# The first expert's tokens and the last pass's results moved by products instead of through memory, in a two-layer diffusion step on one core

## What is computed

```python
for l in range(2):
    xp, xs = layer_norm(ALPHA * x + gate * token_mixers(modulate(x))), ...   # conv and attention, both groups
    h = modulate(x)                                                # h for each group
    f = swiglu(h) if l == 0 else moe_swiglu(h)                     # layer 1: top 2 of 8 experts
    x = layer_norm(ALPHA * x + gate2 * f)

def moe_swiglu(h, router, wg, wu, wd):
    probs = softmax(h @ router); top_v, top_i = top_k(probs, 2); top_v = top_v / sum(top_v)
    gates = sum(one_hot(top_i, 8) * top_v[..., None], axis=-2)
    return sum(gates[..., e] * (silu(h @ wg[e]) * (h @ wu[e])) @ wd[e] for e in range(8))
```

## Time and profile before

| what | value |
|---|---|
| median of 3 runs | 1231.74 us (1231.68 to 1233.32) |
| profiled execution, its time | 1232.15 us |
| its span in the trace | 1230.3 us |
| TensorE (matmul) busy | 1129.3 us, 92% |
| VectorE, ScalarE, GpSimd busy | 852.8, 707.1, 133.7 us |
| moved | 336.78 MB, 274 GB/s |
| mean granted TensorE clock | 0.967 of full speed |

### The profile page before, as it was taken

How to read it: one execution, slowest core, us unless ns; L and a number is a source line. 1 busy time by engine, 2 the same in 40 slices (tenths; PEclk the granted TensorE clock), 3 DMA queues, 4 the chain that set the end, 5 groups by cost and what they waited for, 6 DMA issues and landing times.

```text
span 1230.3 us, 15641 instructions
## 1 busy us (share of the span) xinstructions
PE 1129.3 (92%) x5533; PEld 892.6 (73%) x5533; DVE 852.8 (69%) x1203; ACT 707.1 (57%) x1008; POOL 133.7 (11%) x142
## 2 busy tenths in 40 slices
PE   5699999999999999899999999379999999999980
PEld 1466667887788888766667887368878888888870
DVE  1575657767575455696657676358889889889965
ACT  1444545644644444544545645268888888888862
POOL 5040000001170000440000002220000000000001
PEclk9799999999999999999999999689999999999995
DMA  9799997665469656488775664179999999999952
GB/s 328 278 365 330 318 322 254 203 186 197 140 213 411 222 178 196 132 273 299 261 264 202 215 206 162 57 270 376 375 376 385 377 379 383 379 378 385 376 198 101
DMA packets 167064, 336.78 MB, mean 274 GB/s; under 512 B 6704, under 2 KB 27296, under 8 KB 167008
## 3 DMA queue, kind: packets, MB, share of 16 engines
q1 hardware_dynamic: 158288, 307.78, 71.0%
q0 software_dynamic: 8688, 28.25, 6.7%
q10 hardware_dynamic: 32, 0.01, 0.0%
HBM read 318.68 MB, written 17.33 MB: 273 GB/s over the span
## 4 chain that ended last, share of the span: by engine, by line
PE 84%; ACT 5%; DVE 5%; DMA 3%; issue 2%; POOL 0%; ACTq 0%; SPq 0%; DVEq 0%; POOLq 0%
PE bank L1310 24%; PE bank L1312 24%; PE bank L1311 24%; PE bank L1504 4%; ACT w_hi L568 2%; DMA raw<-in_ada_w 1%; PE bank L1567 1%; PE bank L1585 1%; DVE xT_lo L881 1%; PE bank L1459 1%; PE bank L1575 1%; ACT work L586 1%; DVE w_lo L846 1%; ACT xT_hi L591 1%; PE bank L1448 1%
## 5 line engine op out<-in xcount | busy, mean ns | idle before, releaser
L846 DVE TENSOR_TENSOR w_lo<-raw,w_hi 128x1024 fp32r<-128x1024 f32 (+1 forms) x492 | 571.3, 1190 | 191.7 <-ACT w_hi L568 189.6
L568 ACT ACTIVATE w_hi<-raw 128x1024 fp32r<-128x1024 f32 (+1 forms) x504 | 500.8, 1008 | 314.6 <-PE bank L1312 314.5
L1310 PE MATMUL bank<-w_hi,xT_hi 128*128 128x512 f32 (+1 forms) x1056 | 414.5, 392 | 18.4 <-DVE w_lo L846 12.3
L1312 PE MATMUL bank<-w_lo,xT_hi 128*128 128x512 f32 (+1 forms) x1056 | 403.1, 382 | 0.0
L1311 PE MATMUL bank<-w_hi,xT_lo 128*128 128x512 f32 (+1 forms) x1056 | 402.4, 381 | 0.0
L1310 PEld LDWEIGHTS bank<-w_hi,xT_hi 128*128 128x128 f32 x1056 | 200.4, 190 | 62.4 <-issue 14.2
L1312 PEld LDWEIGHTS bank<-w_lo,xT_hi 128*128 128x128 f32 x1056 | 199.1, 189 | 35.8
L1311 PEld LDWEIGHTS bank<-w_hi,xT_lo 128*128 128x128 f32 x1056 | 199.7, 189 | 31.1
L1310 PE MATMUL bank<-w_hi,hT_hi 128*128 128x512 f32 x360 | 141.8, 394 | 0.0
L1312 PE MATMUL bank<-w_lo,hT_hi 128*128 128x512 f32 x360 | 140.5, 390 | 0.0
L1311 PE MATMUL bank<-w_hi,hT_lo 128*128 128x512 f32 x360 | 140.3, 390 | 0.0
(11 more groups left out here) (236 smaller groups left out, 864.9 us busy)
## 6 DMA issues: line engine op xcount, KB each, us to landing
raw<-in_w_in SPq DMA_DIRECT2D x52, 1024.0 KB, 7.4
raw<-in_ada_w SPq DMA_DIRECT2D x48, 1024.0 KB, 7.5
raw<-in_moe_w_gate SPq DMA_DIRECT2D x32, 1024.0 KB, 7.4
raw<-in_moe_w_up SPq DMA_DIRECT2D x32, 1024.0 KB, 8.0
raw<-in_moe_w_down SPq DMA_DIRECT2D x32, 1024.0 KB, 7.8
raw<-in_moe_w_gate SPq DMA_DIRECT2D x16, 768.0 KB, 8.9
raw<-in_moe_w_up SPq DMA_DIRECT2D x16, 768.0 KB, 7.5
raw<-in_moe_w_down SPq DMA_DIRECT2D x16, 768.0 KB, 7.8
```

The lines of the kernel that those rows point to most:

```text
L568: nc.scalar.activation(w_hi[:, unit, 0:n], raw[:, r, at:at + n], ACT.Copy).then_inc(hi_done, 1)
L846: V.tensor_tensor(w_lo[:, unit, 0:n], raw[:, r, at:at + n], w_hi[:, unit, 0:n].bitcast(F32), ALU.subtract).then_inc(lo_done, 1)
L1310: pe.matmul(o, hi, wh, start=start, stop=False)
L1312: return pe.matmul(o, hi, wl, start=False, stop=stop)
```

## The change

- **First tokens.** Pass 0 no longer reads `x_rows`. A product with ones (`slot_mm`) gives every lane the numbers 1 to 128; VectorE compares them with each token's position in expert 0 (`first_tokens`, before `places`), which gives a 0/1 matrix per group; TensorE multiplies `tokens` by it, 16 products that leave the transposed rows where `gather` left them. The scatter stays, for passes 1 on, and SyncE waits for it three blocks later.
- **Route.** Experts are picked on the logits instead of the probabilities; the two gates follow from one exponential (`gates`), after pass 0's start. The transposes of group 0 go ahead of the router product.
- **Norm before the router.** Group 1's statistics go ahead of group 0's split; VectorE makes the four rests that GpSimd made. In layer 0 and at layer 1's start GpSimd's rests wait until group 0's scales exist.
- **Pass 0** stands ahead of the loop on ScalarE and VectorE too. SyncE takes every expert number from `plan`.
- **Last pass.** The gather of `y_rows` is issued when the pass before has been stored, so it runs beside the last pass; rows of the last pass are zero in memory. A 0/1 matrix times gate (`back_selected`, transposed on TensorE) brings the last pass's rows from `y_slot`: each of four banks takes a product of `best_y` with the identity and one of that matrix with `y_slot`.
- **Last norm and outputs.** Two fused operations per group in place of `xhat` and two; four halves of the output are sent by SyncE, which waits for them.

```diff
                 sp.wait_ge(x_sent, 16 * 2 * G)
-                x_load(0)
                 sp.wait_ge(gx_t, 1)
                 x_load(1)
 
@@ -396,14 +404,19 @@
 
                 expert(p * Q_EXPERT + q, of(e), between)
 
-            expert(q, of(0), first_rows)
-            with sp.Fori(1, NE - 1) as p:
-                one(p, p)
+            expert(q, of(0), first_rows, 2 * SLOTS)
             sp.wait_ge(plan_ok, 1)
             last_pass = sp.value_load(plan[0:1, 0:1], min_val=NE - 1, max_val=PASSES - 1)
-            with sp.Fori(NE - 1, last_pass + 1) as p:
-                one(p, sp.value_load(plan[0:1, bass.ds(p - (NE - 2), 1)], min_val=0, max_val=NE - 1))
-            y_store(last_pass, y_kept)
+            with sp.Fori(1, last_pass) as p:
+                one(p, sp.value_load(plan[0:1, bass.ds(p, 1)], min_val=0, max_val=NE - 1))
+            expert(last_pass * Q_EXPERT + q, of(sp.value_load(plan[0:1, bass.ds(last_pass, 1)], min_val=0, max_val=NE - 1)),
+                   lambda: y_store(last_pass - 1, y_kept))
+            for g in range(G):
+                for half in range(2):
+                    sp.wait_ge(x_ok, 2 * DEPTH + 2 * g + half + 1)
+                    sp.dma_start(out[g][0][:, half * COL:(half + 1) * COL], x[:, g, half * COL:(half + 1) * COL]).then_inc(stored, 16)
+            sp.wait_ge(kv_kept, 64 * DEPTH)
+            sp.wait_ge(stored, 16 * 2 * G)
...
-                rests(turn0[l] + Q_LAYER, 0)
                 if l == 0:
+                    pool.wait_ge(nmr_ok, G + 1)
+                    rests(turn0[l] + Q_LAYER, 0)
...
+                    pool.wait_ge(nmr_ok, G * 2 + 1)
                     rests(turn0[1], 0)
...
                     if j == 8:
-                        act.wait_ge(y_sent, p * 16 + 16)
+                        if last:
+                            act.wait_ge(y_kept, 16)
+                        else:
...
+                    if j == 7 and last:
+                        for g in range(G):
+                            act.wait_ge(y_in[0][g], 16)
+                            nc.scalar.activation(best_y[0][:, g, :], best_y[0][:, g, :], ACT.Copy, scale=rs[:, 3, g:g + 1])\
+                                .then_inc(y_gated, 1)
...
+                    act.wait_ge(slot_mm, 1)
+                    nc.scalar.activation(slot_no, bank[3][:, P:2 * P], ACT.Copy).then_inc(slot_ok, 1)
+                    for i, b in enumerate((6, 7, 4, 5)):
+                        act.wait_ge(xt_t, i + 1)
+                        nc.scalar.activation(tokens[:, i // 2, i % 2 * COL:(i % 2 + 1) * COL], bank[b][:, :], ACT.Copy)\
+                            .then_inc(xt_ok, 1)
...
+                    for i, picked in enumerate((sel_half, gx_t)):
+                        act.wait_ge(picked, 1)
+                        nc.scalar.activation(xT_hi[:, 4 * i:4 * i + 4, 0, :], four(bank[i]), ACT.Copy).then_inc(gx_hi, 1)
+                    one_pass(q0, 0, False)
                     act.wait_ge(plan_ok, 1)
                     last_pass = act.value_load(plan[0:1, 0:1], min_val=NE - 1, max_val=PASSES - 1)
...
+                else:
+                    statistics(1)
+                    modulate(n + 1, 0)
+                    scales(n + 1, 1)
+                    lo(q + 1, 0, (0, 1))
+                    modulate(n + 1, 1)
+                    modulated_rests(n + 1, 0)
                 modulated_rests(n + 1, 1)
...
+            def first_tokens():
+
+                dve.wait_ge(pos_mm, 1)
+                then(V.scalar_tensor_tensor(out=rs[:, 6, :], in0=bank[2][:, 64:64 + G * NE].rearrange("p (g e) -> p g e", g=G)[:, :, 0],
+                                            scalar=1.0, in1=one_hot[:, :, 0], op0=ALU.add, op1=ALU.mult))
+                dve.wait_ge(slot_ok, 1)
+                for g in range(G):
+                    ins = V.tensor_scalar(first_sel[:, g, :], slot_no, rs[:, 6, g:g + 1], None, ALU.is_equal)
+                ins.then_inc(sel_ok, 1)
...
+            def back_selected():
+
+                dve.wait_ge(slot_ok, 1)
+                for i in range(2):
+                    for g in range(G):
+                        ins = V.tensor_scalar(last_terms[:, i, g, :], slot_no, last_rel[:, i, g:g + 1], rs[:, 3 + i, g:g + 1],
+                                              ALU.is_equal, ALU.mult)
+                then(ins)
+                V.tensor_tensor(last_sel, last_terms[:, 0], last_terms[:, 1], ALU.add).then_inc(back_sel, 1)
 
...
+                    V.scalar_tensor_tensor(out=best_y[0][:, g, :], in0=best_y[1][:, g, :], scalar=rs[:, 4, g:g + 1],
+                                           in1=best_y[0][:, g, :], op0=ALU.mult, op1=ALU.add).then_inc(rows_summed, 1)
+                for g in range(G):
+                    for half in range(2):
+                        dve.wait_ge(back_mm, 2 * g + half + 1)
+                        at = slice(half * COL, (half + 1) * COL)
+                        ins = V.tensor_tensor(gate_bc[n % 2][g][:, at], bank[2 * g + half][:, :], gate_bc[n % 2][g][:, at], ALU.mult)
+                    then(ins)
                     then(V.scalar_tensor_tensor(out=x[:, g, :], in0=x[:, g, :], scalar=ALPHA, in1=gate_bc[n % 2][g],
...
+                dve.wait_ge(ld_ln, 32 * (2 * DEPTH + 1))
+                for g in range(G):
+                    dve.wait_ge(std_ok, G * (n + 1) + g + 1)
+                    V.reciprocal(rstd[:, g:g + 1], sd[:, g:g + 1])
+                    then(V.scalar_tensor_tensor(out=x[:, g, :], in0=x[:, g, :], scalar=mv[:, g, 0:1], in1=ln_gb[2 * DEPTH][:, 0, :],
+                                                op0=ALU.subtract, op1=ALU.mult))
+                    for half in range(2):
+                        at = slice(half * COL, (half + 1) * COL)
+                        V.scalar_tensor_tensor(out=x[:, g, at], in0=x[:, g, at], scalar=rstd[:, g:g + 1], in1=ln_gb[2 * DEPTH][:, 1, at],
+                                               op0=ALU.mult, op1=ALU.add).then_inc(x_ok, 1)
...
-                    rests_by_pool(q0, 0)
+                    first_tokens()
                     places()
                     gathered(0)
+                    lo(q0, 0, (2, 3))
+                    gates()
+                    one_pass(q0, 0, False)
                     last_pass = dve.value_load(plan[0:1, 0:1], min_val=NE - 1, max_val=PASSES - 1)
-                    with dve.Fori(0, last_pass) as p:
...
+                    def tokens_turned(g, banks):
+                        pe.wait_ge(mod_hi, G * 3 + g + 1)
+                        for k in range(KD):
+                            ins = pe.transpose(banks[k // 4][:, (k % 4) * T:(k % 4 + 1) * T], modulated[:, g, k, :], ident[:, :])
+                            if k % 4 == 3:
+                                ins.then_inc(xt_t, 1)
+
+                    tokens_turned(0, bank[6:8])
...
+                    idle_products(3, 0)
+                    pe.wait_ge(xt_ok, 2 * G)
+                    pe.wait_ge(sel_ok, 1)
+                    for k in range(KD):
+                        for g in range(G):
+                            ins = pe.matmul(bank[k // 4][:, (k % 4) * T:(k % 4 + 1) * T], tokens[:, g, k * P:(k + 1) * P],
+                                            first_sel[:, g, :], start=g == 0, stop=g == G - 1)
+                        if k == KD // 2 - 1:
+                            ins.then_inc(sel_half, 1)
...
+                    for g in range(G):
+                        pe.wait_ge(rows_summed, g + 1)
+                        for half in range(2):
+                            o = bank[2 * g + half][:, :]
+                            pe.matmul(o, ident[:, :], best_y[0][:, g, half * COL:(half + 1) * COL], start=True, stop=False)
+                            if g == 0:
+                                pe.wait_ge(y_ok, last_pass * 2 + (half + 1))
+                            pe.matmul(o, last_selT[:, g, :], y_slot[:, half * COL:(half + 1) * COL], start=False, stop=True)\
+                                .then_inc(back_mm, 1)
 
```

More of the change, by code:

```diff
@@ L448, in _ @@
                 then(pool.memset(iota[:, v:v + 1], float(v - NE)))
+            for v in range(1, NE):
+                then(pool.memset(plan_f[:, v:v + 1], float(v)))
             then(pool.memset(all_ones[:, :], 1.0))
@@ L540, in _ @@
                                             bass.IndirectOffsetOnAxis(ap=row_no[:, i, g:g + 1], axis=0)).then_inc(y_in[i][g], 16)
-            for g in range(G):
-                pool.wait_ge(x_ok, 2 * DEPTH + g + 1)
-                pool.dma_start(out[g][0], x[:, g, :]).then_inc(stored, 16)
-            pool.wait_ge(stored, 16 * G)
-            pool.wait_ge(kv_kept, 64 * DEPTH)
         @block.scalar
@@ L659, in one_pass @@
                         hi(nq, ns, (0, 1), n)
+                    if j == 2 and last:
+                        act.wait_ge(back_t, 1)
+                        nc.scalar.activation(last_selT, bank[5][:, 0:G * P].rearrange("p (g t) -> p g t", g=G), ACT.Copy)\
+                            .then_inc(back_ok, 1)
```

(32 more changed lines are left out.)

124 lines of the change are left out of this document (63 added, 61 removed).

## The result

The kernel after the change took 1197.31 us (1196.97 to 1200.21, 4 runs), the kernel before 1231.98 us (1231.68 to 1233.32, 4 runs): a ratio of 0.9724, 95% interval 0.9712 to 0.9735. The profiled execution took 1197.48 us, its span is 1195.7 (before 1230.3).

A forecast was written before the change was run, and what follows sets the result against it. TensorE was taken as the bound (47.89 of a 48.3 us pass). Terms -19.6 - 0.7 + 6.2 + 0.5 + 1.0 - 11.6 - 0.5 = -24.7 us gave 1207.0 by the median, own range 1203 to 1211, wider range 1200.5 to 1214.

The forecast's parts named there:

- Pass 0 outside the loop on two engines ... cost nothing visible: Moving pass 0 out of the loop costs nothing visible, since sequencers run ahead; uncovered, some 0.6 us each.
- SyncE's issues cost less than GpSimd's ... 1.0 (0 to 2): End of the span: SyncE's cheaper issues and a last piece of a quarter of the output win 1.0 us.
- Held rests: Two further norms: holding GpSimd's rests until `nmr` wins 0.5 us in all, though delayed rests meet the sum and `xT_lo`.
- Last pass, 0.5 and 1.0: Last pass: compares, sum, copy and transposes cost 0.5 us (0 to 1.5), the gather's transfers 1.0 (0 to 4.2).
- the wait for `raw`: Last pass: a wait for `raw` there was listed among the signs that the forecast is wrong; no size given.
- Norm before the router, route and products: Before pass 0: router product 4.8 us earlier, pass 0 starting at 788.8 against 808.41, 19.6 us earlier (17.5 to 21).
- make_x, 6.2: Pass 0: GpSimd's four operations, no longer covered, alternate with VectorE's rests and lose 6.2 us (0 to 9).
- The rival that the port costs nothing: Pass 0: TensorE keeps going beside make_x, so the 6.2 us loss is absent: 1200.8 us; chance 0.13.
- Warm start, -0.7: Pass 0's start: behind a short gap the first seven products avoid half rate, winning 0.7 us (0 to 1.4).
- Tail on the engines, -10.6: After the last product: VectorE ends at 1210.7 instead of 1221.33, 10.6 us earlier.
- transfers as the bound: Passes: scatter and gather take the weights' time, gather 4.2 us and scatter 1.5 in pass 0: 1211.7; chance 0.12.
- Half clock: Pass 0: beside make_x TensorE's clock halves for the rest of the pass, 34 us lost, 1241; chance 0.03.

The follow-up runs named there:

- e1: The kernel before, with one tiny Silu on ScalarE added ahead of its loop over passes: 1225.60 us, ratio 0.9952.
- e2: The kernel after, with pass 0 put back into the loop on ScalarE alone: 1204.31 us, ratio 0.9773.
- e3: The kernel after, with pass 0 back in ScalarE's loop and one tiny Silu ahead of that loop: 1199.09 us, ratio 0.9737.
- e5: The kernel after, with the four output transfers issued and waited for by GpSimd instead of SyncE: 1205.74 us, ratio 0.9783.
- e7: The kernel after, with outputs still issued by SyncE but waited for by GpSimd: 1202.85 us, ratio 0.9768.
- e4: The kernel after, without the two waits that hold GpSimd's rests: 1193.79 us, ratio 0.9696.
- e11: The kernel after, with SyncE storing the pass before last, which releases the gather, behind all the last pass's weight blocks: 1197.08 us, ratio 0.9721.
- e6: The kernel after, with outputs issued by GpSimd but waited for by SyncE: 1202.75 us, ratio 0.9759.
- e8: The kernel after, without GpSimd's four make_x operations, so the x that the last norm adds to is not computed: 1190.54 us, ratio 0.9662.
- e12: The kernel after, with GpSimd's rests not held, make_x paced in smaller operations and the gather released late: 1191.89 us, ratio 0.9678.
- e10: The kernel after, with make_x in eight operations of 512 columns, each released after another block of rests: 1197.78 us, ratio 0.9713.

## Why the prediction was wrong

The forecast was a gain of 24.7 us, and it was 34.7. The differences by stretch are start +0.7, pass 0 +0.3, six passes -5.95, last pass +1.1, tail on the engines -0.6, end of the span -5.5, together -9.95 beside the -24.7.

- **"Pass 0 outside the loop on two engines ... cost nothing visible"** is the step that failed. It gave 0 to an edit worth 6.0 us: the stretch of six passes fell by 5.95, and with the table loads put in or taken out the period moved by 1.0 us a pass (e1, e2, e3). I asked what the edit costs the sequencers and not what it changes in ScalarE's state at the loop's head. The rows were there to be read: two groups of table loads, seven times each, and 0.4 us of a pass in which TensorE was idle. I had called TensorE the bound at 47.89 of 48.30 us and never asked what the missing part waited for. This miss alone is larger than the 3.2 us by which the time lies below the range.
- **"SyncE's issues cost less than GpSimd's ... 1.0 (0 to 2)"**: 6.5. The term was priced by issue times and the size of the last piece. From GpSimd's last issue to the end of the span it was 8.7 us, while the page gave 2.9 us to the landing. The 5.8 between stood in the profile and belonged to GpSimd (e5 to e7). This miss, too, is larger than 3.2 us by itself.
- **Held rests, "0.5 won in all (bounds: 3 lost, 3 won)"**: 3.5 lost (e4), at the lower bound. That the sum and `xT_lo` would meet the delayed rests was written down; the value near zero was the mistake, for at layer 1's start there was only 0.7 us to win at `nmr` against two such meetings.
- **Last pass, 0.5 and 1.0**: 2.6, within the bounds (0 to 5.7). Some 2.3 of it is the gather's (e11), through ScalarE's waits for weights, the wait for `raw` that was named as a sign of being wrong; moving it does not help.

The other terms:

- **Norm before the router, route and products**: from `nmr` to pass 0's first product 26.4 us, forecast 27.6. The start came out at 789.03 against 788.8 because `nmr` itself began 1.4 us late: 3.5 lost at the holds, less 2.2 by which this execution was early at 70 us. In e5 and e6, whose code is the same up to the outputs, pass 0 starts at 791.45 and 791.19.
- **make_x, 6.2**: near in size, 5.6 (e8; 5.0 with the half clock at the same place, 6.8 by the medians). I had four operations alternating with rests; two of them held up two tiny operations instead. The counting itself came out: until the third stop's end TensorE made 36 products, 8.2 us at 0.23 apart, in 14.9 us, so it was 6.7 us behind a full clock. The rival that the port costs nothing is out.
- **Warm start, -0.7**: not borne out. Pass 0's first products are 0.23 us apart, but the half clock comes all the same, only later: 1.3 us in for 3.6 us in e8, where the stretch has 38.9 us, as before the change, and behind the first stop in the kernel after. Only e12's execution has none.
- **Tail on the engines, -10.6**: -11.2.

Of the other rivals, transfers as the bound came true in the last pass only. Half clock came, for some 7 us and not for the rest of the pass, and with or without `make_x`.

Open is what limits the kernel with `make_x` paced: e10's waits point to the weight transfers, which run at 387 GB/s in a steady pass of the kernel after, but no run took them away. Open is also what decides where in pass 0 the clock falls: the kernel after and e7 have the fall behind the first stop, e2 to e6 and e8 to e11 at the pass's first product or within 2 us of it, and e12 has none.

## What to carry to other kernels

When code moves across a loop's edge, compare the state of each engine at the loop's entry with the one at its end: instructions that only restore state (table loads here) may vanish from, or appear in, every turn. When an edit removes a wait, look first for what that wait was hiding, and book the two as one term. And look at what stands between the last landing and the end of the span: an engine's own end can be longer than the transfer it waits for, and then the last work belongs on another engine.

## What the runs showed of the hardware

- In a loop that needed only Copy and Silu, ScalarE paid two table loads of 1.28 us in each turn, and each turn lost 1.0 us of 48.3, though ScalarE was busy for only 41 us of it. One Silu ahead of the loop ended that (e1).
- Where GpSimd issued or awaited the last transfers, the program's end stood 4.2 (e6), 5.4 (e7) and 6.4 us (e5) further behind VectorE's last operation than with SyncE in both places, where it came with the landing (2.48 us behind VectorE, with 2.1 us of landing).
- VectorE operations on 128 by 2 numbers took 2.37 and 2.22 us beside GpSimd operations of 128 by 1024, each until the GpSimd operation ended, and one between them 0.17: it is not their size that counts but what they have to wait for.
- TensorE's granted clock was at half for 3.6 us in e8 from 1.3 us behind pass 0's first product on, with TensorE never idle there. In e5 the same came at 792.9 to 796.3, and stops of 0.92, 1.66 and 1.67 us behind it left the clock at full. In the kernel after it fell behind a stop of 2.53 us and was back at full at 805.4.
